# Sliding-window attention regrouped by two heads and two query blocks, in a two-layer decoder kernel on one core

## What is computed

```python
def block(args):                      # one of 4 blocks of 128 queries
    qn, kn, vn, ok = args             # its own and the previous key block
    logits = jnp.einsum('bqkgd,bskd->bkgqs', qn, kn) + bias
    logits = jnp.where(ok, logits, -jnp.inf)
    m = jnp.maximum(jnp.max(logits, axis=-1, keepdims=True), sink)
    p = jnp.exp(logits - m)
    denom = jnp.sum(p, axis=-1, keepdims=True) + jnp.exp(sink - m)
    return jnp.einsum('bkgqs,bskd->bqkgd', p / denom, vn)
```

## Time and profile before

| | |
|---|---|
| median of 3 runs | 4215.53 us (4208.02 to 4223.23) |
| the profiled execution | 4224.55 us, of which span 4222.7 us |
| granted TensorE clock, mean | 0.970 |
| busy: PE, DVE, ACT, POOL | 95%, 67%, 36%, 44% of the span |
| DMA | 918.88 MB, mean 218 GB/s |
| attention stage, layer 0 | 341.3 to 533.9 us |
| attention stage, layer 1 | 2429.7 to 2619.4 us |

### The profile page before, as it was taken

How to read it: one execution, slowest core, us unless ns; L and a number is a source line. 1 busy time by engine, 2 the same in 40 slices (tenths; PEclk the granted TensorE clock), 3 DMA queues, 4 the chain that set the end, 5 groups by cost and what they waited for, 6 DMA issues and landing times.

```text
span 4222.7 us, 50008 instructions
## 1 busy us (share of the span) xinstructions
PE 3994.4 (95%) x18106; PEld 3254.1 (77%) x18106; DVE 2819.9 (67%) x4288; ACT 1524.6 (36%) x2217; POOL 1841.4 (44%) x956
## 2 busy tenths in 40 slices
PE   5899988999999999999998999999899999999999
PEld 4667777877877887888876777778778878788887
DVE  3135654798988946888733366158898988488886
ACT  2434523333333333333335344233333333333332
POOL 2322233344434447777423221433344444477772
PEclk9999899999999999999999998999999999999999
DMA  7436874243445459999834377553335444799996
GB/s 255 141 130 221 302 292 143 91 144 112 169 161 197 171 209 347 379 349 354 307 128 143 110 277 246 170 186 113 125 127 207 159 162 171 257 386 353 352 355 206
DMA packets 412179, 918.88 MB, mean 218 GB/s; under 512 B 38736, under 2 KB 176848, under 8 KB 410352
## 3 DMA queue, kind: packets, MB, share of 16 engines
q1 hardware_dynamic: 328368, 664.98, 45.5%
q0 software_dynamic: 45056, 134.38, 8.6%
q10 hardware_dynamic: 38592, 117.46, 7.1%
HBM read 794.00 MB, written 256.90 MB: 249 GB/s over the span
## 4 chain that ended last, share of the span: by engine, by line
PE 79%; issue 7%; DVE 6%; POOL 3%; ACT 3%; DMA 1%; SPq 1%; POOLq 0%; ACTq 0%; DVEq 0%
PE ps L894 13%; PE ps L895 13%; PE ps L896 13%; PE ps L909 10%; PE ps L911 10%; PE ps L910 10%; POOL w_lo L848 3%; PE ps L1201 2%; PE ps L1085 1%; DMA raw<-in_stream_dram 1%; DVE raw L1279 1%; PE ps L1093 1%; PE ps L1106 1%; ACT w_hi L530 1%; SPq L409 0%
## 5 line engine op out<-in xcount | busy, mean ns | idle before, releaser
L848 POOL TENSOR_TENSOR w_lo<-raw,w_hi 128x1024 fp32r<-128x1024 f32 x440 | 1128.3, 2565 | 2024.1 <-ACT w_hi L530 2024.1
L530 ACT ACTIVATE w_hi<-raw 128x1024 fp32r<-128x1024 f32 x504 | 534.1, 1060 | 1849.3 <-PE ps L896 1355.3
L894 PE MATMUL ps<-h_hi,w_hi 128*128 128x512 f32 x2880 | 1140.4, 396 | 7.9 <-DVE idxT L1547 7.7
L895 PE MATMUL ps<-h_hi,w_lo 128*128 128x512 f32 x2880 | 1132.1, 393 | 0.0
L896 PE MATMUL ps<-h_lo,w_hi 128*128 128x512 f32 x2880 | 1129.9, 392 | 0.0
L894 PEld LDWEIGHTS ps<-h_hi,w_hi 128*128 128x128 f32 x2880 | 546.4, 190 | 127.6 <-issue 16.4
L896 PEld LDWEIGHTS ps<-h_lo,w_hi 128*128 128x128 f32 x2880 | 545.0, 189 | 119.0
L895 PEld LDWEIGHTS ps<-h_hi,w_lo 128*128 128x128 f32 x2880 | 545.9, 190 | 106.9
L861 POOL DMA_INDIRECT down<-expert_down,e_row x256 | 336.2, 1313 | 216.1 <-DVE ps L1672 94.8
L1619 DVE TENSOR_TENSOR hot_i<-same_i,pick 128x1024 fp32r<-128x1024 f32 x192 | 423.4, 2205 | 0.0
L853 POOL DMA_INDIRECT acts<-expert_act,e_act x256 | 376.7, 1471 | 103.6 <-issue 77.4
(11 more groups left out here) (253 smaller groups left out, 5981.0 us busy)
## 6 DMA issues: line engine op xcount, KB each, us to landing
raw<-in_stream_dram SPq DMA_DIRECT2D x648, 512.0 KB, 3.3
expert_down<-in_stream_dram SPq DMA_DIRECT2D x256, 512.0 KB, 5.8
expert_act<-gel ACTq DMA_DIRECT2D x256, 256.0 KB, 2.0
raw_more<-in_stream_dram SPq DMA_DIRECT2D x128, 512.0 KB
expert_gate<-gatebuf ACTq DMA_DIRECT2D x12, 4096.0 KB, 12.5
a_in<-expert_act SPq DMA_DIRECT2D x128, 384.0 KB
g_in<-expert_gate SPq DMA_DIRECT2D x128, 384.0 KB
ada_first<-in_stream_dram SPq DMA_DIRECT2D x16, 512.0 KB, 13.0
```

Source lines behind the costliest of these rows:

```text
L530: return act.activation(o, i, ACT.Copy)
L848: pool.tensor_tensor(w_lo[:, s, :], raw[:, b, :], w_hi[:, s, :].bitcast(F32), ALU.subtract).then_inc(lo_ready, 1)
L894: pe.matmul(o, w_hi[:, s, w], mov_hi[:, c, :], start=c == 0, stop=False)
L895: pe.matmul(o, w_lo[:, s, w], mov_hi[:, c, :], start=False, stop=False)
```

## The change

The unit of attention work becomes an item: heads 2g and 2g + 1 for two of the four query blocks, i = 2g + half, 16 items as there were 16 heads.

- Scores: the two heads of an item lie in partitions 0 to 63 and 64 to 127, and their matmuls alternate between the row halves of the array, into two PSUM banks.
- Values: the value matrix becomes the stationary operand and the probabilities move; the two heads' results go to PSUM partitions 0 to 63 and 64 to 127. They come out transposed, so that `o_s`, its 32 transposes and DVE's scaling are gone, and `ob_hi` and `ob_lo` are made per pair of heads within the loop.
- Probabilities are divided by the denominator before they are transposed: ACT waits for `den_ready` of DVE and does 4 copies with a scale (`scale`). DVE forms the denominator of item i at the end of its turn i (before: two heads later).
- PE transposes item i - 1 and multiplies the values of item i - 2 in turn i; `logit` has three buffers instead of two.
- The 12 weight units within the loop stand at the turns that `FILL` names: none at i = 3, 7, 11, 15. The list follows: each item's two "a" units, and a "w" unit only where `FILL` has one; `U_MIXB` and `U_MIXB + 1` come behind the last item. ACT still splits unit m + 2 after unit m.
- SP loads the bias tables for two heads at a time, the first of them ahead of the stream's loads; the norm roots have ten bank places instead of six, and the first scores wait for 3 roots, not 8.

```diff
+FILL = [None if _i % 4 == 3 else U_MIXA + 4 + _i - _i // 4 for _i in range(SH)]
+
 ORDER_OF = []
 for _l in range(DEPTH):
     _o = [("w", m) for m in range(U_MIXA + 4)]
-    for _h in range(SH):
-        _o += [("a", N_ADA1 + 2 * _h), ("a", N_ADA1 + 2 * _h + 1)] + ([("w", U_MIXA + 4 + _h)] if _h < 14 else [])
+    for _i in range(SH):
+        _o += [("a", N_ADA1 + 2 * _i), ("a", N_ADA1 + 2 * _i + 1)] + ([("w", FILL[_i])] if FILL[_i] else [])
+    _o += [("w", U_MIXB), ("w", U_MIXB + 1)]
...
+                load_listed(l, swa, swa + RAW)
+                at_item = swa + RAW
+                for g in range(SH // 2 - 2):
+                    count = 4 + sum(FILL[i] is not None for i in (2 * g, 2 * g + 1))
+                    load_listed(l, at_item, at_item + count)
+                    at_item += count
+                    sp.wait_ge(bias_free, l * 13 + 2 * g + 3)
+                    load_bias(2 * g + 4)
+                    load_bias(2 * g + 5)
...
+                def soften(i):
+                    w, lg = 80 + 12 * (i % 4), logits_of(i)
+                    act.wait_ge(logit_ready, l * SH + i + 1)
...
+                def scale(i):
+                    w, lg = 80 + 12 * (i % 4), logits_of(i)
+                    act.wait_ge(den_ready, l * SH + i + 1)
+                    for r in range(4):
+                        ins = act.activation(lg[:, r, :], lg[:, r, :], ACT.Copy, scale=small[:, w + 4 + r:w + 5 + r])
+                    ins.then_inc(scaled, 1)
+
+                def keep_ob(g):
+                    act.wait_ge(os_mm, l * SH + 2 * g + 2)
+                    copy(ob_hi[:, g, :], ps[:, 2 + g % 2, :]).then_inc(tr_hi, 1)
...
+                after_unit(l, U_MIXA + 2)
+                soften(0)
+                scale(0)
+                for i in range(SH + 1):
+                    if i == 0:
+                        after_unit(l, U_MIXA + 3)
+                    elif FILL[i - 1]:
+                        after_unit(l, FILL[i - 1])
+                    if i:
+                        keep_pT(i - 1)
+                    if i >= 4 and i % 2 == 0:
+                        keep_ob(i // 2 - 2)
+                    if i + 1 < SH:
+                        soften(i + 1)
+                        scale(i + 1)
+                after_unit(l, U_MIXB)
+                keep_ob(SH // 2 - 1)
```

```diff
+                def logits(i):
+                    g, half = divmod(i, 2)
+                    if i:
+                        pe.wait_ge(logit_ready, l * SH + i)
+                    for b in (2 * half, 2 * half + 1):
+                        for hh in range(2):
+                            r, o = slice(HD * hh, HD * hh + HD), ps[:, 4 + hh, b % 2 * 256:b % 2 * 256 + 256]
+                            q = qT_s[r, g, b * P:(b + 1) * P]
+                            if b == 0:
+                                mm = pe.matmul(o[:, 128:256], q, kT_s[r, g // 4, 0:P], start=True, stop=True)
+                            else:
+                                mm = pe.matmul(o, q, kT_s[r, g // 4, (b - 1) * P:(b + 1) * P], start=True, stop=True)
...
+                def probs(i):
+                    pe.wait_ge(scaled, l * SH + i + 1)
+                    if i:
+                        pe.wait_ge(pT_ready, l * SH + i)
+                    lg = logits_of(i)
+                    for hh in range(2):
+                        for j in range(1 - i % 2, 4):
+                            mm = pe.transpose(ps[:, 6 + hh, j * P:j * P + P],
+                                              lg[:, 2 * hh + j // 2, j % 2 * P:j % 2 * P + P], ident)
...
+                def values(i):
+                    g, half = divmod(i, 2)
+                    pe.wait_ge(pT_ready, l * SH + i + 1)
+                    if half == 0 and g >= 2:
+                        pe.wait_ge(tr_done, l * 2 * KC + KC + g - 1)
+                    kv = slice(g // 4 * HD, g // 4 * HD + HD)
+                    for b in (2 * half, 2 * half + 1):
+                        for side in range(0 if b else 1, 2):
+                            for hh in range(2):
+                                o = ps[HD * hh:HD * hh + HD, 2 + g % 2, b * P:b * P + P]
+                                mm = pe.matmul(o, v_s[:, b - 1 + side, kv], pT[:, i % 2, 4 * hh + b % 2 * 2 + side, :],
+                                               start=side == 0 or b == 0, stop=side == 1, skip_group_check=True)
                     mm.then_inc(os_mm, 1)
...
+                for i in range(SH + 2):
+                    if i == 1:
+                        pe.wait_ge(sqk_ready, l * 10 + 10)
+                    if i + 1 < SH:
+                        logits(i + 1)
+                    if 1 <= i <= SH:
+                        probs(i - 1)
+                    if i < SH and FILL[i]:
+                        unit(l, FILL[i])
+                    if i == SH:
+                        unit(l, U_MIXB)
+                    if i >= 2:
+                        values(i - 2)
```

```diff
+                for i in range(SH):
+                    (g, half), lg = divmod(i, 2), logits_of(i).rearrange("p (a b) c -> p a b c", a=2)
+                    lp = ps[:, 4:6, :].rearrange("p a (b c) -> p a b c", b=2)
+                    bias = bias_s[:, g % 2 * 2:g % 2 * 2 + 2, :]
+                    dve.wait_ge(logit_mm, l * SH + i + 1)
...
+                    else:
+                        step(tt_op(lg, lp, bias.unsqueeze(2).to_broadcast([P, 2, 2, 256]), ALU.add))
+                        if g < SH // 2 - 2:
+                            dve.sem_inc(bias_free, 2)
...
+                    ins.then_inc(logit_ready, 1)
...
+                    streamed_modulation(l, N_ADA1 + 2 * i)
+                    streamed_modulation(l, N_ADA1 + 2 * i + 1)
+                    done = U_MIXA + 3 if i == 1 else FILL[i - 2] if i >= 2 else None
+                    if done and (done - U_MIXA) % 2:
+                        gated_a(l, (done - U_MIXA) // 2)
+                    if i >= 6 and half == 0:
+                        ob_lower(g - 3)
+                    dve.wait_ge(prob_ready, l * SH + i + 1)
+                    den = small[:, w + 4:w + 8]
+                    step(tt_op(den, den, small[:, w + 8:w + 12], ALU.add))
+                    dve.reciprocal(den, den).then_inc(den_ready, 1)
+                gated_a(l, 7)
+                for g in range(5, KC):
+                    ob_lower(g)
```

More of the change, by code:

```diff
@@ L724, in _ @@
-                keep_pT(SH - 1)
-                transposed_hi(ob_hi, l * 2 * KC + KC)
-                for m in range(U_MIXB, U_OUT):
+                after_unit(l, U_MIXA + 2)
[13 more added lines that the diff above has]
+                        scale(i + 1)
@@ L727, in _ @@
+                after_unit(l, U_MIXB)
+                keep_ob(SH // 2 - 1)
+                for m in range(U_MIXB + 1, U_OUT):
                     after_unit(l, m)
@@ L1115, in _ @@
                 roots(8, 10)
-                pe.wait_ge(sqk_ready, l * 10 + 10)
-                for h in range(SH):
-                    if h < SH - 1:
-                        logits(h + 1)
-                    probs(h)
-                    if h < 12:
-                        unit(l, U_MIXA + 4 + h)
-                    if h:
-                        values(h - 1)
-                unit(l, U_MIXB)
-                values(SH - 1)
-                pe.wait_ge(os_ready, (l + 1) * SH)
-                transposed(o_s, l * 2 * KC + KC)
+                for i in range(SH + 2):
[9 more added lines that the diff above has]
+                        unit(l, U_MIXB)
+                    if i >= 2:
+                        values(i - 2)
                 for m in range(U_MIXB + 1, U_OUT):
```

154 lines of the change are left out of this document (48 added, 106 removed).

## The result

| | before | after |
|---|---|---|
| median of 4 runs each, same comparison | 4219.38 us (4208.02 to 4228.29) | 4272.34 us (4266.04 to 4277.88) |
| ratio, 95% interval | | 1.0123 (1.0100 to 1.0145) |
| profiled execution, of which span | 4224.55, 4222.7 | 4271.33, 4269.5 |
| granted TensorE clock, mean | 0.970 | 0.963 |
| attention stage, layer 0 | 341.3 to 533.9 = 192.7 | 340.4 to 560.4 = 220.0 |

The changed kernel is 1.2% slower. The last three lines say more than the first: the stages grew by 27.3 and 30.9 us, 58.2 together, and the rest of the program became 11.4 us shorter.

What follows compares the result with a forecast made beforehand. PE bounded the kernel before; a circle of waits through loads, ACT and DVE would take over. Layer 0 adds 20 us, layer 1 23, 45 in all: 4224.6 becomes about 4270, median 9 lower, 4260 (4218 to 4300).

Steps and rivals of the forecast that it cites:

- The step from 4270 to 4260: Whole program: the median of the runs was taken as 9 us below the profiled execution.
- its lower bound: Whole program: with loads of 4.0 us and no allowance, 25 us in all, giving 4240.
- The circle, its place and its period: Attention stage: load, ACT's split and exponential, and DVE wait in turn; groups of four items take 46.6 and 50.4 us.
- The load leg: Attention stage, part of the circle: an awaited weight load takes 4.5 us, bounds 4.0 and 7.0.
- the 546 of the sum: Layer 0's attention stage: start, groups of four items and end, added from 341.3, finish at 546 us before allowance.
- The 8 us of allowance: Layer 0's attention stage: 8 us added for PE at 1.2 GHz after waits and occasional 7 us loads, giving 554.
- What follows the stage: After the attention stage: modulation, diagonals and mixing units keep their order and move along.
- Array shapes: PE in the attention stage: a change of array shape costs 0.1 us at most, counted as nothing.
- It works as intended: Rival, attention stage: weights land before ACT wants them; stage 152 us, or 168 if DMA bounds; total 4136 to 4172; 11%.
- Only one leg bites: Rival, attention stage: second and third kinds of split find units landed; no change, 4205 to 4228 us; 8%.
- The low clock decides: Rival, attention stage: units after waits run wholly at 1.2 GHz, 45 us more, 4305; 11%.
- The halves do not overlap: Rival, PE in the attention stage: PE lacks its 22 us, costing 3 us a layer, 4266; counted within the forecast.

Runs made afterwards that it cites:

- e12: Changed kernel, but ACT scales one of an item's four rows of probabilities instead of four: 4273.7 us, one run.
- e6: Changed kernel, but the store-to-store copies of the down weights in the attention's stretch are issued after the queries' loads: 4354.1 us, one run.
- e10: Changed kernel with fill units and load list as in the kernel before, and DVE's denominator taken one turn later: 4158.2 us, ratio 0.9841 to before.
- e5: Changed kernel, but scores and values of one head come before those of the other instead of alternating: 4272.1 us, one run.
- e8: Changed kernel, two of each three weight units one item earlier in the load list, DVE using "a" units one item ahead: 4170.3 us, ratio 0.9881 to before.
- e9: Changed kernel with fill units and load list as in the kernel before, and DVE using "a" units one item ahead: 4163.4 us, ratio 0.9862 to before.
- e13: e10 with DVE also using the "a" units one item ahead: 4191.0 us, ratio 0.9931 to before.

## Why the prediction was right

It said 4260 (4218 to 4300), slower with 81%; it came out at 4272.34. Against the profiled execution it said about 4270, and that is 4271.33. The mechanism is the one it named. But its sum meets the result partly by luck, through errors that cancel: the stages grew by 58.2 us where the sum had 45 in all, and the rest of the program shrank by 11.4 where it had nothing, which leaves 46.8. The step from 4270 to 4260 also failed: the profiled execution of the changed kernel lies 1 us below its median and not 9 us above it. And its lower bound does not follow from its terms: nine loads of 4.0 and no allowance, in two layers, leave 45 - 9 - 16 = 20 us, 4235, where it says 25 and 4240.

- **The circle, its place and its period.** Right. DVE waits for its own exponential in 15 turns, ACT before splits in 12 places (the profile wrote "issue" where I had foreseen DMA; in e12 it names the load), PE before pT in 8 with 10.6 at the longest, a little over the 5 to 9 foreseen. DMA share 0.57 to 0.72 in the three stretches, under the 0.8 given. From the split at 390.55 to that at 494.08, two groups of four, are 103.5 us; the sum had 97.
- **The load leg.** This term was mis-sized, and its reason was wrong. I took 4.5 us, "since the queues will be emptier than at 368". The ten legs on the path, from the issue of a load to the split, take 9.1 (366.00 to 375.08), 3.4 (387.19 to 390.55), 6.3, 6.0, 6.1, 6.8, 7.3, 3.5, 6.0 and 6.9 (523.57 to 530.46): 61.2 us where ten times 4.5 are due. The queues are emptier on average, but the loads come in bursts, because DVE, once it is free, uses two "a" units directly one after the other. The leg at 387.19 begins its burst, the one at 400.44 stands second in it:

```profile
387.19 0.34 SPq L393 DMA_DIRECT2D raw<-in_stream_dram  x1
387.57 0.54 SPq L416 DMA_DIRECT2D expert_down<-in_stream_dram  x1
...
390.55 1.06 ACT L540 ACTIVATE w_hi<-raw 128x1024 fp32r<-128x1024 f32 x1 [5.67 <-issue]
...
399.30 0.33 SPq L393 DMA_DIRECT2D raw<-in_stream_dram  x1
399.68 0.54 SPq L416 DMA_DIRECT2D expert_down<-in_stream_dram  x1
...
400.44 0.41 SPq L393 DMA_DIRECT2D raw<-in_stream_dram  x1
```

  Both have their own copy of 512 KB issued right behind them. The first load landed after 3.3 us, the second after 6.2. A copy beside does not by itself make a load late; what differs is the load and the copy issued 1.1 us ahead. The ten legs cost 16 us more than the sum had, against 14 between the 546 of the sum and the measured 560.4; the other terms gave 2 back. The 8 us of allowance stood in for half of it, and the stage came out at 220.0 against 213. In e6, with the copies gone, the ten legs take 45.7, and its stage of 204.3 meets the 204.7 that the sum had before the allowance.
- **The second layer.** 213 predicted, 220.6 measured; the same term.
- **What follows the stage.** "Keeps its order and moves along": this step was wrong by 11.4 us, the other way. From the end of layer 0's stage to the start of layer 1's the time fell from 1895.7 to 1888.8 us, and from the end of layer 1's to the end by 3.6. In the mixing section after layer 0's stage (145.5 us before, 139.4 after) PE's wait for the diagonals fell from 4.0 to 0.4 us, and the granted clock was 0.98 instead of 0.95. I take the first to be because DVE has no output to scale at the end of the stage, which no run shows by itself. Every version of the changed kernel but e6 shows 3824 to 3836 outside the stages, and both forms of the kernel before 3840 and 3844, so the gain belongs to the change. What it is made of beyond those 3.6 us was not tested.
- **Scores, values, copies.** 1.06 and 0.86 us from start to start in the two halves, mean 0.96 (0.9 predicted); values 1.02 and 0.81 (1.0 predicted). After long waits the granted clock was 0.50 to 0.53, and the same groups took up to 2.08 and 1.96 us. Scaled copies 1.7 (1.6 predicted). PE's busy time of the stage fell from 177.9 to 149.6 us, 28 less, "some 30" predicted.
- **Array shapes.** The three rows of PE above are column halves, row halves and full width; each group starts 0.07 to 0.24 us before the one ahead of it is shown to end (426.79, 427.81, 428.88, and the next unit at 429.73). I saw no gap of a matmul's length there. The rule that I set aside (the Trainium skill, TensorEngine Tiling (Array Packing), Key Properties) says that a change of mode drains the engine and gives no price; the 27 us a layer were my estimate for a drain of one matmul. These rows leave no such gaps.
- **Table loads.** In the pass at 406.72 the split ends at 407.78, the load runs from 407.79 to 409.07 and the sigmoid starts at 409.08: a switch of tables costs 1.3 us here, the term I used. The Trainium skill, ScalarE: Activation LUTs, section What ACT_TABLE_LOAD costs, adds a drain of 1.38 us to the load's 1.28; this trace agrees on the load and shows no such drain.
- **The rivals.** *It works as intended*: in the profile of the changed kernel, no. But e10 reached stages of 159 to 161 us, inside the 152 to 168 worked out for it, and 4158, inside its 4136 to 4172. The condition named for it, "where weights land before ACT wants them", is just what e10 provides. *Only one leg bites*: no, three splits in each group wait. *The low clock decides*: clock 0.82 in the stage instead of 0.89, but ACT's splits wait for PE only at the two ends of the stage, and the load legs account for the end without it. *The halves do not overlap*: they do; and that PE's pairing matters little on this path was borne out by e5, for the values.

## What to carry to other kernels

When a change alters how many units of work go between two weights, move the list of loads with it: for each consumer write down in which turn it wants its unit and which use of the ring issues that load; if the use comes from an engine that waits for this consumer, the saving turns into a circle. A circle's price is the sum of its legs and not anyone's busy time, so work on an arc where an engine waits anyway is free (e12) and a shorter transfer on it counts at every turn (e6). A transfer's time depends on what is still in flight when it is issued, and a load that a circle waits for is better off as the first of its burst: the two such legs here took 3.4 and 3.5 us, the others 6.0 to 9.1. No version that puts it there on purpose was tried. Letting one consumer of a shared ring run ahead helped twice (e8, e9) and cost 18 to 21 us a layer on top of the fastest version (e13), so it is to be measured each time.

## What the runs showed of the hardware

- Two row halves overlap without alternating one by one: eight score records of 256 columns took 1.14 us alternating by matmul and 1.14 in runs of four records, 1.07 from start to start in both, where the kernel before, with all of them on one row half, took 1.72 from start to start for six of 256 columns and two of 128. With column halves, 16 value records took 1.09 alternating by matmul, 1.14 in runs of four records, 1.58 in runs of eight. Scores in runs of eight were not tried, so it is open whether row and column halves differ or only the length of the run decides.
- The same 512 KB load took 4.4 us from issue to landing (median of 47) with no copies in the stage and 6.7 with a copy of 512 KB issued behind each, at a mean DMA share of only 0.45 and 0.66. What was issued ahead counts for most of it. Of the loads of the changed kernel's stage from 359 us on, the eight issued with no other load in flight landed after 3.2 to 3.4 us although a copy followed each within 0.4 us; the eleven with one load in flight took 3.4 to 7.2, the 20 with two 6.0 to 10.0. In e6, without the copies, a load with none in flight took 3.0 to 3.7 and one with one in flight 3.4 to 5.6. A mean share under one does not say that a transfer lands at its unloaded time.
